# Encoder trunk kernel: loads of x, gates, scale and unit rows asked for when their space comes free, with eight value buffers and four key buffers

## The reference, cut to what matters

```python
h = modulate(x, norm1_gain, sh1, sc1)          # RMSNorm, scale, shift
z = h @ w_in                                   # gq gk gv gr glr dq dk dv gates
o_a, gla_state = gla_recurrence(q, k, v, log_a, h0)
k_rows, v_rows = rope(rmsnorm(dk)), dv         # outputs, and keys/values of attention
o_b = diff_attend(q1, q2, k1, k2, v_rows, mask, lam)
mix = (sigmoid(g_a) * y_a + sigmoid(g_b) * y_b) @ w_out
x = x + gt1 * mix
h2 = modulate(x, norm2_gain, sh2, sc2)
idx, g = top16 of (h2 @ w_pq) against sub_keys   # 8 heads x 16 experts per token
act = gelu(einsum('td,thkd->thk', h2, peer_u[idx]))
x = x + gt2 * einsum('thk,thkd->td', g * act, peer_v[idx])
```

## Time and profile before

| | |
|---|---|
| median of 3 runs | 4300.85 us (4298.69 to 4303.13) |
| span of the profiled execution, which is all its page gives of its own time | 4303.9 us |
| PE busy | 3099.8 us (72%) |
| DVE busy | 2705.5 us (63%) |
| ACT busy | 1511.1 us (35%) |
| moved by DMA | 1499.17 MB, 1107.36 MB of it gathers |

### The profile page before, as it was taken

One profiled execution on the slowest core, in us unless ns is written; L12 is line 12 of the kernel. 1 busy time (PEld: TensorE's weight loads), 2 busy tenths in 40 slices (PEclk: granted clock), 3 DMA queues, 4 the chain that ended last, 5 costly groups with the idle time before them and its releaser, 6 DMA issues. The chain is left out here.

```text
span 4303.9 us, 48708 instructions
## 1 busy us (share of the span) xinstructions
PE 3099.8 (72%) x15864; PEld 1982.7 (46%) x15864; DVE 2705.5 (63%) x7617; ACT 1511.1 (35%) x3085; POOL 1254.2 (29%) x1068
## 2 busy tenths in 40 slices
PE   6787798887788769778887679768776677733333
PEld 4676565665555337455554347444433254400000
DVE  1326357337667884477668873577678945776775
ACT  3533366312255651114555540223446611010010
POOL 0000111112233332333223332333334323355553
PEclk8888888898888779898888889888778788855555
DMA  7485767687989989998999899989999999999998
GB/s 261 157 305 189 278 243 267 254 319 307 357 343 375 360 309 390 404 415 354 363 362 366 351 359 384 417 344 402 375 372 386 363 410 415 398 408 415 416 406 336
DMA packets 269363, 1499.17 MB, mean 348 GB/s; under 512 B 44968, under 2 KB 81672, under 8 KB 97464
## 3 DMA queue, kind: packets, MB, share of 16 engines
q0 software_dynamic: 152064, 1107.36, 64.5%
q1 hardware_dynamic: 117048, 388.70, 24.0%
HBM read 1463.49 MB, written 31.36 MB: 347 GB/s over the span
## 5 line engine op out<-in xcount | busy, mean ns | idle before, releaser
L1698 POOL DMA_INDIRECT rt_ring<-in_peer_uv,rt_few_idx x1056 | 1250.9, 1185 | 3021.0 <-PE rt_acc L876 2385.5
L1644 DVE SCALAR_TENSOR_TENSOR rt_ring<-rt_ring,rt_h 128x1024 f32<-128x1024 f32 x1056 | 1265.9, 1220 | 504.7 <-DMA rt_ring<-in_peer_uv,rt_few_idx 481.7
L876 PE MATMUL rt_acc<-rt_ring,rt_diag 128*32 128x512 f32 x4224 | 759.9, 795 | 623.1 <-DVE rt_diag L1655 622.1
L625 PE MATMUL pair<-dense,w 128*128 128x256 f32 (+2 forms) x3056 | 598.6, 355 | 14.0 <-DMA w<-in_weights 12.2
L625 PEld LDWEIGHTS pair<-dense,w 128*128 128x128 f32 x3056 | 518.1, 199 | 128.8 <-issue 64.5
L614 PE MATMUL pair<-w,dense 128*128 128x256 f32 (+1 forms) x2352 | 556.4, 395 | 9.5 <-DVE dense L1300 3.5
L1199 ACT ACTIVATE rt_act_dot<-rt_dot 128x2 f32<-128x2 f32 x528 | 106.1, 202 | 1269.0 <-DVE rt_ring L1644 1262.1
L876 PEld LDWEIGHTS rt_acc<-rt_ring,rt_diag 128*32 128x32 f32 x4224 | 100.1, 122 | 953.4 <-DVE rt_diag L1655 810.1
L614 PEld LDWEIGHTS pair<-w,dense 128*128 128x128 f32 (+1 forms) x2352 | 436.2, 189 | 158.8 <-issue 72.9
L1655 DVE TENSOR_SCALAR rt_diag<-cst,rt_act_dot,rt_few_prob 128x32 f32<-128x32 f32 x1056 | 266.1, 296 | 119.9 <-ACT rt_act_dot L1199 109.5
L625 PE MATMUL bank<-dense,w 128*128 128x256 f32 (+2 forms) x1424 | 276.9, 351 | 1.7 <-DMA w<-in_weights 1.2
(11 more groups left out here) (241 smaller groups left out, 3248.5 us busy)
## 6 DMA issues: line engine op xcount, KB each, us to landing
w<-in_weights SPq DMA_DIRECT2D x284, 1024.0 KB
rt_ring<-in_peer_uv,rt_few_idx POOLq DMA_INDIRECT x1056
dense<-scratch_mod SPq DMA_DIRECT2D x18, 512.0 KB, 12.4
dense<-in_x_prompt SPq DMA_DIRECT2D x16, 512.0 KB, 13.5
rt_h<-scratch_h SPq DMA_DIRECT2D x33, 128.0 KB
rt_x<-scratch_x SPq DMA_DIRECT2D x132, 32.0 KB
out_k_prompt<-dense SPq DMA_DIRECT2D x32, 128.0 KB
out_v_prompt<-dense SPq DMA_DIRECT2D x32, 128.0 KB
```

Source lines behind the costliest of these rows:

```text
L625: mm = nc.tensor.matmul(bank[b][:, 0:n], wt[:, k * CH + j * P:k * CH + (j + 1) * P], src[:, k, 0:n], start=(k == 0), stop=(k == KC - 1))
L876: mm = nc.tensor.matmul(acc[u % 2][a * T:(a + 1) * T, :], diag[b % 2][:, i, :], slot[:, D + c * BANK:D + (c + 1) * BANK], start=(q == 0), ...
L1644: dt = nc.vector.scalar_tensor_tensor(up, up, 1.0, h2[u % 2][:], ALU.mult, ALU.mult, accum_out=dot[:, b % 2, i:i + 1])
L1698: nc.gpsimd.indirect_dma_start(ring[n % RING][:], None, d["peer_uv"], bass.IndirectOffsetOnAxis(ap=few_idx[u % 2][:, c:c + 1], axis=0)).th ...
```

## The change

Four things change, on the SP queue and in the arena; no arithmetic is changed.

1. `load_x` of group g+1 moves from the last tick of `keys` to the first, and waits for the shifted tiles of group g in place of the last key projection.
2. The gate rows and the scale row are asked for at merge tick 2, once the attention output is copied, and x at merge tick 30, once the last two projections that read `hT` are done. The scale row lies in the unused second half of `gate1` for groups 0 to 3; in group 4, which needs both gate rows, it keeps its place and stays at tick 32.
3. `unit(u)` asks for the h2 rows before it waits for the expert numbers.
4. `kst` becomes four buffers and `vst` eight; the waits on their stores follow. ACT gets a new wait before it first writes the log-decays, which share space with the fourth key buffer.

```diff
+VBUF, KBUF = 8, 4
...
-        kst, vst = area(6144, 4 * NCOL, 2, 2), area(7168, 3 * CH, 3)
+        kst = [area(start, 2 * NCOL, 2) for start in (6144, 6656, 7168, 8192)]
+        vst = area(2048, VBUF * CH, VBUF)
...
+        def values_stored(g, i):
+            return (4 * (FIRST[g] + len(GROUPS[g])) + VBUF - 1 - i) // VBUF
+
+        def scale_of(g):
+            return scale2 if NT in GROUPS[g] else gate1[:, 1, :]
...
-                            act.wait_ge(kt_out[k % 2], 16 * (k // 2))
-                            dst = kst[:, k % 2, j, 0:n]
+                            act.wait_ge(kt_out[k % KBUF], 16 * (k // KBUF))
+                            dst = kst[k % KBUF][:, j, 0:n]
...
-                    act.wait_ge(v_out[v % 3], 32 * (v // 3))
+                    act.wait_ge(v_out[v % VBUF], 32 * (v // VBUF))
...
             def decay_logs(g, p, j):
+                if h == 0:
+                    act.wait_ge(kt_out[KBUF - 1], 16 * (g + 1))
...
             def load_x(t):
                 if g > 0:
-                    b, before = sessions["kq", g - 1, PH - 1, 1]
-                    sp.wait_ge(bank_made[b], before + 1)
+                    sp.wait_ge(mx_shifted, FIRST[g])
...
             def merge(g, i):
-                if i < 32:
-                    return
-                b, before = sessions["mg", g, 31]
-                sp.wait_ge(bank_made[b], before + 1)
-                for ti, t, c0, n in places(g):
-                    src = d["x_prompt"][0, t * P:(t + 1) * P] if t < NT else d["x_sample"][0]
-                    sp.dma_start(x1[0:n, ti, :], src).then_inc(x1_in, 16)
-                sp.wait_ge(mg_done, 8 * (g + 1))
-                for i in range(2):
-                    sp.wait_ge(md_out[i], 128)
-                for s in sorted({stream(t) for t in GROUPS[g]}):
-                    sp.dma_start(gate1[:, s, :], d["mod"][s:s + 1, 0:D].to_broadcast([P, D])).then_inc(gate_in, 16)
-                sp.dma_start(scale2, d["mod"][0:1, 2 * D:3 * D].to_broadcast([P, D])).then_inc(scale_in, 16)
+                if i == 2:
+                    sp.wait_ge(at_copied, ATTEND[g][3])
+                    for k in range(2):
+                        sp.wait_ge(md_out[k], 128)
+                    for s in sorted({stream(t) for t in GROUPS[g]}):
+                        sp.dma_start(gate1[:, s, :], d["mod"][s:s + 1, 0:D].to_broadcast([P, D])).then_inc(gate_in, 16)
+                    if NT not in GROUPS[g]:
+                        sp.dma_start(scale_of(g), d["mod"][0:1, 2 * D:3 * D].to_broadcast([P, D])).then_inc(scale_in, 16)
+                if i == 30:
+                    for k in (28, 29):
+                        b, before = sessions["mg", g, k]
+                        sp.wait_ge(bank_made[b], before + 1)
+                    for ti, t, c0, n in places(g):
+                        src = d["x_prompt"][0, t * P:(t + 1) * P] if t < NT else d["x_sample"][0]
+                        sp.dma_start(x1[0:n, ti, :], src).then_inc(x1_in, 16)
+                if i == 32 and NT in GROUPS[g]:
+                    sp.wait_ge(mg_done, 8 * (g + 1))
+                    sp.dma_start(scale2, d["mod"][0:1, 2 * D:3 * D].to_broadcast([P, D])).then_inc(scale_in, 16)
...
             def keys(g, h, i):
-                if h == PH + 1 and g + 1 < NG:
+                if h == 0 and i == 0 and g + 1 < NG:
                     for t in GROUPS[g + 1][:2]:
                         load_x(t)
...
             def unit(u):
+                for k in range(2):
+                    sp.wait_ge(h2_out[k], 16 * sum(s % 2 == k for s in range(GROUPS[g][-1] + 1)))
+                sp.wait_ge(x1_out, 16 * (GROUPS[g][-1] + 1))
+                sp.dma_start(h2[i][0:T, :], d["h2"][row:row + T]).then_inc(tokens_in[i], 16)
                 sp.wait_ge(idx_ready, t + 1)
...
-                for k in range(2):
-                    sp.wait_ge(h2_out[k], 16 * sum(s % 2 == k for s in range(GROUPS[g][-1] + 1)))
-                sp.wait_ge(x1_out, 16 * (GROUPS[g][-1] + 1))
-                sp.dma_start(h2[i][0:T, :], d["h2"][row:row + T]).then_inc(tokens_in[i], 16)
```

More of the change, by code:

```diff
@@ L479, in trunk @@
         kr_out = [sem(f"rp_kr_out{i}") for i in range(3)]
-        kt_out = [sem(f"rp_kt_out{i}") for i in range(2)]
-        v_out = [sem(f"dv_out{i}") for i in range(3)]
+        kt_out = [sem(f"rp_kt_out{i}") for i in range(KBUF)]
+        v_out = [sem(f"dv_out{i}") for i in range(VBUF)]
         la_logged, la_ready = sems("la", "logged ready")
@@ L1004, in dv @@
                     act.wait_ge(bank_made[b], before + 1)
-                    act.wait_ge(v_out[v % 3], 32 * (v // 3))
-                    nc.scalar.activation(vst[0:n, v % 3, :], bank[b][0:n, 0:CH], ACT.Copy).then_inc(bank_free[b], 1)
+                    act.wait_ge(v_out[v % VBUF], 32 * (v // VBUF))
+                    nc.scalar.activation(vst[0:n, v % VBUF, :], bank[b][0:n, 0:CH], ACT.Copy).then_inc(bank_free[b], 1)
             def place_qk(kind, g, p, j):
@@ L1053, in gla_v @@
                     if u == 0 and p == 0:
-                        for i in range(2):
-                            act.wait_ge(kt_out[i], 16 * 2 * (g + 1))
+                        for i in range(KBUF):
+                            act.wait_ge(kt_out[i], 16 * (g + 1))
                     act.wait_ge(bank_made[b], before + 1)
@@ L1085, in gla @@
                             act.wait_ge(kr_out[i], 16 * max(rows_stored(r) for r in range(g * 8 + 4) if r % 3 == i))
-                            act.wait_ge(v_out[i], 32 * ((4 * FIRST[g] + 4 * len(GROUPS[g]) + 2 - i) // 3))
+                        for i in range(VBUF):
+                            act.wait_ge(v_out[i], 32 * values_stored(g, i))
                     act.wait_ge(gl_blocked, base + k + 1)
@@ L1382, in gla @@
                             dve.wait_ge(kr_out[i], 16 * max(rows_stored(r) for r in range(g * 8 + 4) if r % 3 == i))
-                        for i in range(2):
-                            dve.wait_ge(kt_out[i], 16 * 2 * (g + 1))
+                        for i in range(KBUF):
+                            dve.wait_ge(kt_out[i], 16 * (g + 1))
                         settle(nc.vector.memset(k_blk, 0.0))
@@ L1541, in shift @@
                 dve.wait_ge(scale_in, 16 * (g + 1 + stream(t)))
-                settle(nc.vector.scalar_tensor_tensor(h2b[t % 2][0:n, :], x1[0:n, ti, :], mrstd[0:n, ti:ti + 1], scale2[0:n, :],
+                settle(nc.vector.scalar_tensor_tensor(h2b[t % 2][0:n, :], x1[0:n, ti, :], mrstd[0:n, ti:ti + 1], scale_of(g)[0:n, :],
                                                       ALU.mult, ALU.mult))
@@ L1726, in stored @@
             def stored(g):
-                nv = 4 * (FIRST[g] + len(GROUPS[g]))
-                for i in range(3):
-                    sp.wait_ge(v_out[i], 32 * ((nv + 2 - i) // 3))
-                for i in range(2):
-                    sp.wait_ge(kt_out[i], 16 * 2 * (g + 1))
+                for i in range(VBUF):
+                    sp.wait_ge(v_out[i], 32 * values_stored(g, i))
+                for i in range(KBUF):
+                    sp.wait_ge(kt_out[i], 16 * (g + 1))
             def load_x(t):
@@ L1797, in rotary @@
                     sp.dma_start(d["kT"][2 * i:2 * i + 2, :, c:c + n].rearrange("h p t -> p h t"),
-                                 kst[:, k % 2, :, 0:n]).then_inc(kt_out[k % 2], 16)
+                                 kst[k % KBUF][:, :, 0:n]).then_inc(kt_out[k % KBUF], 16)
             def dv(g, tick):
@@ L1808, in dv @@
                     dst = d["v_prompt"][0, 0, t * P:(t + 1) * P] if t < NT else d["v_sample"][0, 0]
-                    sp.dma_start(dst[:, 2 * i:2 * i + 2, :].rearrange("t h v -> t (h v)"), vst[0:n, v % 3, :]).then_inc(v_out[v % 3], 16)
+                    sp.dma_start(dst[:, 2 * i:2 * i + 2, :].rearrange("t h v -> t (h v)"), vst[0:n, v % VBUF, :]).then_inc(v_out[v % VBUF], 16)
                     sp.dma_start(d["vh"][2 * i:2 * i + 2, 0:n, t * VD:(t + 1) * VD].rearrange("h p c -> p h c"),
-                                 vst[0:n, v % 3, :].rearrange("p (h c) -> p h c", h=2)).then_inc(v_out[v % 3], 16)
+                                 vst[0:n, v % VBUF, :].rearrange("p (h c) -> p h c", h=2)).then_inc(v_out[v % VBUF], 16)
             def store_state(g, p):
```

## The result

| | before | changed |
|---|---|---|
| median of the runs | 4301.99 us (4298.69 to 4305.71) | 4261.2 us (4250.27 to 4265.75) |
| ratio | | 0.9896, 95% interval 0.9879 to 0.9914 |
| profiled execution, span | 4303.9 us | 4262.5 us |
| granted clock, mean | 0.801 | 0.802 |
| PE / DVE / ACT busy | as given ahead | 3112.3 / 2708.3 / 1513.0 us |

By the ratio the change is faster by 44.7 us (37 to 52); the medians, of four runs each, differ by 40.8 us. A second set of five runs of the same kernel on another occasion gave 0.9912 (0.9895 to 0.9929); the two together stand near 0.9904, 41 us. One of the runs of the kernel before that were made beside the experiments had a granted clock of 0.573 and took 5218.67 us; it is left out everywhere. The forecast was 4259, in a range of 4230 to 4284. The total was right.

The account below looks back on a forecast made before the run. Engines' order was taken to bound the kernel early, nearly full DMA engines later. Terms 11.6 + 12.8 + 12.0 + 0.6 + 2.5 + 2 = 41.5 us gave 4259 us, range 4230 to 4284.

Parts of the forecast that it names:

- Which regime, and which waits count: Whole kernel: engines' order sets the pace early, nearly full DMA engines later, where stalls cost only what DMA loses.
- Group 2, 11.6 us: Norm of group 2: the whole 11.61 us wait for x counts, taken as 11.6 us, lower bound 10.2.
- Groups 3 and 4, 12.8 and 12.0: Norms of groups 3 and 4: only idle DMA time counts, 12.8 and 12.0 us, upper bounds 20.6 and 20.7.
- The same bytes move: Keys: 1 MB of x shares the engines with gathers at the start instead of the end; no net gain or loss.
- rival B: Norms: another wait stands close behind x, so half of each gap returns; gain 20 us, 4281 us, chance 0.13.
- h2, 2.5 us: Unit 0 of the expert stage: the first pair of dot products ends 2.5 us sooner; bounds 0 and 4.4.
- Value buffers, 2 us: dv stages: most of ACT's 86.0 us of waits are covered; one visible 4.85 us stall in group 2, taken as 2.
- Rows for mix, 0: Mix: DVE catches up after its 9.36 us wait for gate rows, 0 us; shift row 0 to 5.5, taken as 0.
- Rival A: Norms of groups 3 and 4: the whole wait counts, 20.6 + 20.7 us; total gain 66 us, 4235 us, chance 0.20.
- Rival C: Whole kernel: DMA engines alone set the pace, or loads do not go early; 0 to 8 us, chance 0.04.
- Rival D: Merge stages, groups 2 to 4: rows delay weight tiles, nine times 9.7 us, 87 us; ends near 4346, chance 0.03.
- the bound of 20: Behind 1000 us: PE waits for weight tiles adding up to over 20 us would show the forecast wrong.

Follow-up runs that it names:

- e4: Kernel before with gate and scale rows asked for at merge tick 2 and x1 at tick 30, nothing else; ratio 0.9968, 14 us faster.
- e1: Kernel before with only the next group's x asked for at the first tick of keys instead of its last; ratio 0.9922, 34 us faster.
- e8: Kernel before with x at the start of keys and gate, scale and x1 rows early, old buffers and h2; ratio 0.9904, 41 us faster.
- e9: Kernel before with x asked for somewhat earlier, still late in keys, 16 us ahead of use; ratio 0.9914, 37 us faster.

## Why the prediction came out right

- **Which regime, and which waits count.** Right. Of the waits that the change removes, 86.0 us for value stores brought a lead that was gone some steps later, and nothing that shows in the time; 58.7 us for x brought nearly all.
- **Group 2, 11.6 us.** Too much: 7.3 to 8.5. The failed step is "What stays of PE's stall is the chain from ACT's square to PE's transposes, 5.1 us". It is 7.7 us: PE's stalls went from 14.50 + 1.91 to 7.66 + 0.28, so by 8.5, which is the ledger's step to the tenth. Here as in group 3, DVE's selection was hidden under the wait for x and came out when that went: DVE had idled 6.75 us before its scale in group 2, and has no wait there now. In groups 3 and 4 the stall that I had announced, 5 to 8 us, is 6.49 and 8.52.
- **Groups 3 and 4, 12.8 and 12.0.** Too little: 16.5 and 17.2. The failed step is "between 1935 and 1960 their share is 0.49, so 25 x 0.51 = 12.8 us": a share over a window that ends before the gap does. Counted in bytes to the end of the refill it is 15.3 and 17.7, or 14.8 and 16.3 against the lower rates behind the gaps.
- **"The same bytes move ... nothing gained or lost in sum."** Nearly. The norms give 41.0 us, the timed kernels with x alone 34 to 39; the ledger has 6.3 us less in two later stretches, inside its scatter, and some 9 us less over the whole. If that is real, it is rival B's mechanism at a fifth, not at a half. B's 20 us lie below the interval of the change and of each kernel with x early.
- **h2, 2.5 us.** 1.15 at the first gelu, gone 32 steps later. The failed step is the pair's end, 450.2 + 1.2: the second product's gather was not in yet, and the pair ended 15.6 us after the numbers, 452.8 on that clock.
- **Value buffers, 2 us.** Between -1 and 8, so not refuted; but the mechanism was a swap, 4.85 us of waiting for a slot against 5.21 for a weight tile.
- **Rows for mix, 0.** Wrong as a pair (7 to 20 us by e4), not refuted for either alone. I had argued that DVE catches up behind the first product. What failed in that is open, since no trace shows where the pair gains. The sum had no term for it and none for what the norms lose again, it had too much for group 2 and h2 and too little for groups 3 and 4. That these errors cancelled was luck.
- **Rival A** (the whole wait, 4235) is ruled out by e1's interval. **Rival C** (the DMA engines alone, at most 8 us, which is 4293 and not the 4295 that I wrote) is ruled out by every kernel with x early. The slices of the changed kernel read 413 to 417 GB/s in seven of forty. The Trainium skill (DMA: Bandwidth & Descriptors, Specifications) gives about 358 GB/s as a core's limit of HBM; as a limit that does not hold for this kernel, which runs on one core. **Rival D** (weight tiles late) exists at a small size. PE's waits for weight tiles behind 1000 us add up to 24.6 us, over the bound of 20 that I had set as a sign of error. That bound was badly set, since the kernel before has 12.1 us already; 10.6 us are the two waits that came with the value buffers, and e8, with the rows early and the old buffers, has 13.6.

## What to carry to other kernels

A wait hides the work of other engines as well as its own: before pricing its removal, list what they do meanwhile and put it back behind. A gap of a saturated resource is counted in what it failed to move until it is full again, not in the busy share of a window. And when one execution is compared with another step by step, kernels without the edit must stand beside them: the 2.3 us at the first unit, half of the 4 us behind group 1's mix and half of the loss in the attention of group 3 looked like effects of the change and belong to single executions. Two places of comparison must be tried, too: a loss of 5 us at one step was 2 to 3 us a few steps on.

## What was unexpected of the hardware

How long a load of x takes depends on more than how full the DMA engines are. In the kernel before, the first half of x landed 22.6 and 23.5 us after its request in groups 3 and 4, and 11.9 us after it in group 2 (requests at 1915.53, 2839.13 and 1028.30). The DMA share over these times was 0.99, 0.99 and 1.01. The six other kernels with x late show the same: 22.4 to 23.9 us and 9.7 to 11.9 us. What stood ahead on SP's queue differs. In groups 3 and 4 the loads of a unit, a weight tile and the y stores had gone out within the 13 us before, in group 2 weight tiles alone. In e9, where x goes out ahead of the unit's loads and right behind a weight tile, it took at most 15.7 us in group 3. So the small loads and stores ahead may be what makes 12 us into 23; no run moved them alone, and that is not shown. And with no edit at all, leaving out the one run at a clock of 0.573, the kernel's time spans 4290 to 4316 us, 0.6%, over the other 63 runs on three occasions, with a mean granted clock between 0.796 and 0.805.
